# One layer of a chunk-causal encoder on one core: sums of a gathered tile move from the output phase to the gate phase, and the first loads and the last normalisation are placed anew

## The reference

```python
s = einsum('thpd,hpkd->thpk', q, sub_keys)          # 8 heads, 2 halves, 128 keys
sv, si = top_k(s, 16)                               # then the 16 best of 256 sums
idx = i1 * 128 + i2 ; g = softmax(best sums)        # 8 x 16 experts for each token
a = g * gelu(einsum('tkd,td->tk', expert_u[idx], x))
out = einsum('tk,tkd->td', a, expert_v[idx])
```

## Time and profile before

| | us |
|---|---|
| median of three runs (lowest, highest) | 3660.91 (3656.52, 3666.24) |
| the profiled execution's own time | 3626.26 |
| its span | 3624.5 |

### The profile page before, as it was taken

One profiled execution on the slowest core, in us unless ns is written; L12 is line 12 of the kernel. 1 busy time (PEld: TensorE's weight loads), 2 busy tenths in 40 slices (PEclk: granted clock), 3 DMA queues, 4 the chain that ended last, 5 costly groups with the idle time before them and its releaser, 6 DMA issues. The chain is left out here.

```text
span 3624.5 us, 42794 instructions
## 1 busy us (share of the span) xinstructions
PE 3096.4 (85%) x16184; PEld 2401.6 (66%) x16184; DVE 2127.5 (59%) x4487; ACT 1195.0 (33%) x1931; POOL 1474.7 (41%) x1116
## 2 busy tenths in 40 slices
PE   4995989798879999999999998666468988999994
PEld 3874777677768778888777766444246656677773
DVE  4143774215432169888867776767366666655555
ACT  3212452304221143444333332887422212222221
POOL 3100002410210007555867677776545545433332
PEclk9997699899989999999999999888779999999997
DMA  4333003321322249988999999899999999999993
GB/s 157 103 100 131 1 14 127 116 87 53 134 87 71 61 167 409 347 333 326 409 410 410 409 411 406 326 396 392 394 329 360 362 354 354 365 325 323 324 324 137
DMA packets 368045, 937.45 MB, mean 259 GB/s; under 512 B 31440, under 2 KB 130264, under 8 KB 366816
## 3 DMA queue, kind: packets, MB, share of 16 engines
q0 software_dynamic: 147456, 536.94, 38.6%
q1 hardware_dynamic: 220384, 397.77, 30.9%
HBM read 827.60 MB, written 106.98 MB: 258 GB/s over the span
## 5 line engine op out<-in xcount | busy, mean ns | idle before, releaser
L1406 POOL DMA_INDIRECT ex_ring<-in_expert_v,ex_idxT_sb x406 | 468.9, 1155 | 429.1 <-PE ex_ps_v L1431 300.0
L1406 POOL DMA_INDIRECT ex_ring<-in_expert_u,ex_idx_sb x322 | 428.0, 1329 | 386.9 <-DVE ex_hg L1415 205.1
L1415 DVE CUSTOM_DVE_ANT_0 ex_ring<-ex_ring,ex_xg 128x1024 f32<-128x1024 f32 x322 | 385.0, 1220 | 118.9 <-DMA ex_ring<-in_expert_u,ex_idx_sb 117.7
L106 PE MATMUL eo_ps<-eo_v_hi_sb,aT_late_hi 128*128 128x512 f32 x1024 | 410.7, 401 | 28.1 <-DVE aT_late_lo L1979 28.1
L106 PE MATMUL ex_ps_h<-aT_late_hi,ex_uT_hi_sb 128*128 128x512 f32 x1024 | 412.6, 403 | 1.9 <-ACT ex_uT_lo_sb L1547 1.1
L107 PE MATMUL eo_ps<-eo_v_lo_sb,aT_late_hi 128*128 128x512 f32 x1024 | 402.8, 393 | 0.0
L108 PE MATMUL ex_ps_h<-aT_late_hi,ex_uT_lo_sb 128*128 128x512 f32 x1024 | 402.1, 393 | 0.0
L107 PE MATMUL ex_ps_h<-aT_late_lo,ex_uT_hi_sb 128*128 128x512 f32 x1024 | 401.2, 392 | 0.0
L108 PE MATMUL eo_ps<-eo_v_hi_sb,aT_late_lo 128*128 128x512 f32 x1024 | 401.1, 392 | 0.0
L1431 PE MATMUL ex_ps_v<-ex_ring,ex_w_sb 128*32 128x512 f32 x1624 | 266.4, 697 | 147.4 <-DMA ex_ring<-in_expert_v,ex_idxT_sb 118.7
L1986 DVE TENSOR_TENSOR eo_acc<-eo_acc,eo_ps 128x1024 f32<-128x1024 f32 x124 | 151.5, 1221 | 356.9 <-PE eo_ps L108 356.9
(11 more groups left out here) (328 smaller groups left out, 6609.7 us busy)
## 6 DMA issues: line engine op xcount, KB each, us to landing
ex_u_raw<-in_expert_u SPq DMA_DIRECT2D x128, 512.0 KB, 8.3
eo_v_raw<-in_expert_v SPq DMA_DIRECT2D x128, 512.0 KB, 6.6
act_d<-ex_act SPq DMA_DIRECT2D x128, 256.0 KB, 6.1
gate_d<-ex_gate SPq DMA_DIRECT2D x8, 4096.0 KB, 14.9
eo_g_raw<-gate_d SPq DMA_DIRECT2D x64, 512.0 KB, 6.7
eo_a_raw<-act_d SPq DMA_DIRECT2D x128, 256.0 KB, 5.4
h_d<-n_row SPq DMA_DIRECT2D x24, 512.0 KB, 2.6
pin_raw<-in_w_in SPq DMA_DIRECT2D x20, 512.0 KB, 3.9
```

The source lines that it names most:

```text
L106: pe.matmul(ps, l_hi, r_hi, start=first, stop=False)
L1406: pool.indirect_dma_start(rows(n), None, table, bass.IndirectOffsetOnAxis(at, 0)).then_inc(ring_in[slot[n]], 16)
L1415: dve.tensor_tensor_reduce(out=u, in0=u, in1=xg[:, j, :], scale=1.0, scalar=0.0, op0=ALU.mult, op1=ALU.add, accum_out=hg[:, j, k:k + 1]).t ...
```

## The change

Counts and places are new, no arithmetic is. In words:

- Expert phase: the first tile's indices are computed in step 8 (`picked`, cut out of `route`), and dots begin at step 9, not 12. The weights of the softmax stay where they were.
- Gate phase: 96 steps instead of 72, still 64 of them with gate work. The 64 dots lie in steps 0 to 39, tile 1's 32 values in steps 0 to 45, the turn to tile 2 in steps 44 to 50 (`TURN_G` = 48), and tile 2's 32 values, formerly in the output phase, in steps 50 to 95.
- Output phase: 96 dots in e = 0 to 59; no values before e = 68, and tile 3's 32 values in e = 68 to 111. The first four experts' rows are loaded without a wait, the v rows into `acc`, the activations into the two `v_raw` buffers. The residual rows are loaded in e = 4 to 7 into `acc`, and added by the first group's `add`.
- The four gathered tiles are normalised within groups 30 and 31. Behind the last matmul only the late tiles are left, each after its own `add`. Gain and bias go into ring slots.

```diff
-            STEPS_G = HOT_GROUPS + 8
+            STEPS_G, TURN_G = HOT_GROUPS + 32, 48
-            FIRST_DOT = 12
+            FIRST_DOT = 9
             DOTS_A, DOTS_G, DOTS_B = 352, 64, 96
-            VALS_A, VALS_G, VALS_B = P, P, 2 * P
+            VALS_A, VALS_G, VALS_B = P, 2 * P, P
+            LAST_VALS, LN_TILES = 112, GROUPS - 2
+            def dots_g(n):
+                first = 2 * (DOTS_G // 2)
+                return share(first, TURN_G - 8, n) if n < TURN_G - 8 else 0
+            def vals_g(n):
+                if n < TURN_G - 2:
+                    return share(P // 4, TURN_G - 2, n)
+                if n >= TURN_G + 2:
+                    return share(P // 4, STEPS_G - TURN_G - 2, n - TURN_G - 2)
+                return 0
+            def dots_b(e):
+                return share(DOTS_B, ETILES // 2 - 4, e) if e < ETILES // 2 - 4 else 0
+            def vals_b(e):
+                half = ETILES // 2
+                if half + GE <= e < LAST_VALS:
+                    return share(P // 4, LAST_VALS - half - GE, e - half - GE)
+                return 0
...
     def a_raw(e):
-        return a_sb[:, e % 2, :]
+        return v_sb[:, e // 2, e % 2 * DN:(e % 2 + 1) * DN] if e < GE else a_sb[:, e % 2, :]
     def v_raw(e):
-        return v_sb[:, e % 2, :]
+        return acc[:, e, :] if e < GE else v_sb[:, e % 2, :]
...
+    for e in range(GE):
+        sp.dma_start(v_raw(e), v_rows[e, :, :]).then_inc(first_in[e], 16)
+        sp.dma_start(a_raw(e), act_d[e, :, :]).then_inc(first_in[e], 16)
+        if e % 2 == 0:
+            load_gates(e // 2)
...
+        if e < 2 * GE:
+            t = e - GE
+            sp.wait_ge(v_lo_done, t + 1)
+            sp.dma_start(acc[:, t, :], resid[(GT + t) * P:(GT + t + 1) * P, :]).then_inc(row_in[t], 16)
...
     if q == 0:
-        dve.tensor_copy(acc[:, t, :], ps[t % 2][:])
+        dve.wait_ge(row_in[t], 16)
+        dve.scalar_tensor_tensor(acc[:, t, :], acc[:, t, :], ALPHA, ps[t % 2][:], ALU.mult, ALU.add)
...
+    if LN_TILES <= q < LN_TILES + GT // 2:
+        j = 2 * (q - LN_TILES) + x // 2
+        if x % 2 == 0:
+            dve.wait_ge(sum_g, j + 1)
+            ln.statistics(dve, j, whole_row(j))
+        else:
+            ln.scale(dve, j)
+        if x % 2 == 0 and j >= 1:
+            ln.times_gain(dve, j - 1, whole_row(j - 1))
...
+    for t in range(DT):
+        add(GROUPS - 1, t)
+        dve.wait_ge(added[t % 2], 2 * (GROUPS - 1) + t // 2 + 1)
+        ln.statistics(dve, GT + t, whole_row(GT + t))
+        ln.times_gain(dve, GT + t - 1, whole_row(GT + t - 1))
+        ln.scale(dve, GT + t)
```

More of the change, by code:

```diff
@@ L1311, in expert_stages @@
             for n in range(STEPS_G):
-                for _ in range(share(DOTS_G, STEPS_G, n)):
+                for _ in range(dots_g(n)):
                     gathers.append(("u", nu))
                     nu += 1
-                for _ in range(4 * share(VALS_G // 4, STEPS_G, n)):
+                for _ in range(4 * vals_g(n)):
                     gathers.append(("v", nv))
@@ L1368, in expert_stages @@
             row_in = [sem(f"eo_row_in{i}") for i in range(DT)]
-            sum_done, stored = sem("eo_sum"), sem("eo_stored")
+            first_in = [sem(f"eo_first_in{i}") for i in range(GE)]
+            stored = sem("eo_stored")
             with ExitStack() as whole:
@@ L1855, in _ @@
                                         one_hot(n + 2)
-                                    for _ in range(share(DOTS_G, STEPS_G, n)):
+                                    for _ in range(dots_g(n)):
                                         dot(dve, done)
                                         done += 1
-                                weigh(dve, 2)
+                                    if n == TURN_G - 3:
+                                        weigh(dve, 2)
+                                    if n == TURN_G:
+                                        add_residual(dve, 1)
+                                        spread_weights(dve, 2)
                             @block.tensor
@@ L1878, in _ @@
                                         gates(n)
-                                    for _ in range(share(VALS_G // 4, STEPS_G, n)):
+                                    if n == TURN_G:
+                                        weight_transpose(pe, 2)
+                                    for _ in range(vals_g(n)):
                                         values(pe, done)
@@ L1884, in expert_stages @@
                     sb, pb = local(stage)
-                    ln = RowNorm("eo_ln", sb, gain, bias, rows=(spreads[:, 0, :], spreads[:, 1, :]))
+                    ln = RowNorm("eo_ln", sb, gain, bias, rows=(ring[:, 0, :], ring[:, 1, :]))
                     acc = sb("eo_acc", [P, DT, D])
@@ L1929, in _ @@
+                                if e == LN_TILES * GE:
                                     sp.wait_ge(val_done, GT * P // 4)
@@ L1994, in _ @@
                                 for x in range(GE):
[L1995 to L1997 removed]
+                                    multiply(q * GE + x)
+                                    low_parts(q * GE + x)
                                     if q >= 1:
                                         add(q - 1, x)
[L2000 to L2003 removed]
+                                    for _ in range(dots_b(q * GE + x)):
+                                        dot(dve, done)
+                                        done += 1
@@ L2043, in _ @@
                                     last.then_inc(out_mm[t % 2], 1)
-                                    for _ in range(share(VALS_B // 4, ETILES, q * GE + t)):
+                                    for _ in range(vals_b(q * GE + t)):
                                         values(pe, done)
```

109 lines of the change are left out of this document (50 added, 59 removed).

## The result

Timed side by side on the chip, 20 executions each, the changed kernel took 3667.07 us (median; 3654.97 to 3687.74) and the kernel before 3657.43 (3641.0 to 3670.12). The ratio over these executions is 1.0039, 95% interval 1.0022 to 1.0057, which is 14 us slower (8 to 21; the two medians alone lie 9.6 apart), where 9.5 us faster was forecast. A second comparison gave 1.0033 (1.0017 to 1.0049), 12 us.

The account below looks back on a forecast made before the run. DMA bytes bound the later expert phase and the gate phase, TensorE the output phase's second half. Expert -6, gate +164, output -132 and end -35.5 sum to -9.5: 3651 us against the median, range 3620 to 3690.

Parts of the forecast that it names:

- the price of the gate phase: Gate phase: 128 added gathers each cost their bytes, 1.28 us at 410 GB/s, +163.8 us, taken as +164.
- as at 391: Gate phase: bound of +172 us if every byte costs as at 391 GB/s.
- The third rival: Gate phase: tile 2's values wait for slots; at 6.4 us a set 28 more, +18, 3679 us; chance 0.13.
- The +14: Whole kernel, if the DMA limit were about 358 GB/s: 1.46 us a gather, gate phase +187; no chance of its own.
- The turn: Gate phase, steps 46 to 49 without values: ScalarE takes 16 to 18 us, the DMA has 22 us of work.
- The last two groups: End of the output phase: normalisation adds 3.4 us to VectorE in two steps, 10.5 of 11.15; 1 us added.
- The fourth rival: Groups 30 and 31: normalisation does not hide; at 2 us a tile lost, +8, so -1.5, 3659 us; chance 0.06.
- the output phase's first 15 groups: Groups 0 to 14: VectorE level with TensorE, 22.9 us a group, 343.5 us; bounds 22.3 and 25.7.
- the second rival: Output phase: the two raw buffers bind from a landing of 7.8; with 9.5, +42, so +32, 3693 us; chance 0.11.
- The end: Behind the last matmul: 13.3 us instead of 48.8, difference -35.5.
- The start: Output phase start: first matmul 26 us after the first issue, between 20 and 29, where it was 28.6.
- waits of values in triples: Output phase, groups 17 to 27: values wait for v gathers, 1.5 us short in each of 8 triples, +12; bounds 0 and 35.

Follow-up runs that it names:

- after2: The changed kernel, unchanged, run again for a second trace; ratio 1.0033 to the kernel before.

## Why the prediction was wrong, step by step

**The step that failed is the price of the gate phase:** "Since the DMA is saturated there, each costs its bytes: 1.28 us at 410 GB/s, +163.8". The growth was 179 us in the mean of all traces (183 by those of the first table, 168 to 194 by single pairs), 1.40 a gather, at the upper bound of 180.

The evidence for saturation was a DMA share of 1.00, but the rate beside it was 391 and not 410, and I priced the added bytes at the rate of another phase. The missing 5% was lost time, not other work's bytes. Over the whole phase, 2260.9 to 2620.7, the kernel before moved 377 GB/s; 67.1 MB at that rate are 178 us. The changed phase ran at about the same rate, 366 to 379 and some 375 in the mean, so its losses grew with its bytes.

That the stores' bursts and the slots are part of them is shown by the experiments; how, is my reading: behind a store the 13 slots land late and together, and the DMA has less to do until they are spread again. My bound "as at 391" (+172) took one window, without the phase's beginning and end, and the loss in it as constant; in that window the changed kernel ran at 370 to 383. By the timed ratios 14 slots give 14 us back, dots in the turn 7 (inside the intervals), both together 15, and pieces another 19; with all three the price is 164.

The third rival, slots, had the right kind of loss, at 28 us instead of some 14. (Its worse case, 7.7 us a set, is 57 us above the forecast, so +47 in all, and not the +57 that stands there.) The +14 that the prediction works out from a lower limit of the DMA is the measured figure by chance: the whole gate phase moved 366 GB/s or more in every trace with 13 slots, and 398 with pieces.

**The turn** was reckoned to have DMA work throughout, 22 us of it against 16 to 18 for four steps. I had miscounted the steps: `share(32, 46, 0)` is 0, so step 50 has no set of values either, and from the last set of tile 1, in step 45, to the first of tile 2, in step 51, TensorE's list has the gate work of six steps (46 to 51). ScalarE, which paces them at some 4.1 us each, was busy 20.0 of the 20 us from 2620 to 2640. The gap was 26 us (2606 to 2632), and 23 to 24 in the other four traces of the same phase; GpSimd was cut off for 19.3 us of it, and the DMA ran dry for 6 to 7 (share 0.28 from 2625 to 2635; 0.30 from 2608 to 2617 in after2). I had given such a gap 8 us in the bound only, which was its size.

**The last two groups:** "I add 1 for it". It was 11 to 14 (96 us by the adds, where 84.5 and 81.6 are had). The fourth rival had the place right, VectorE's list with waits on ScalarE, and the price at 8; that ScalarE's list holds back the high part, and that the bias addition on GpSimd stretches a low part by 2.15 us, I had not seen. The first could have been read from the order of ScalarE's list. The second stood in my rows, misread: the sum of 3.27 us at 3609.15 began 0.16 us after an addition of GpSimd that I had not put beside it,

```profile
3608.99 2.35 POOL L217 TENSOR_TENSOR eo_acc<-eo_acc,ex_w_sb 128x1024 f32<-128x1024 f32 x1 [4.18 <-DVE eo_acc L211]
```

and ended 1.08 us behind it, as the stretched low parts do. All four sums of 3.27 us lie so. I had put their length down to the product's place in SBUF instead of PSUM; an operation with both inputs in SBUF takes 1.22 as well where GpSimd makes no such addition (L1977 in the earlier trace rows).

**Right:** the output phase's first 15 groups were 347.8 us between the adds of group 0 and 15, first step at the low clock included (343.5 predicted; 344 to 353 in the other traces with the move), with VectorE level with TensorE as reckoned. The loads into two raw buffers did not bind; v rows landed in 7.0 us median in after2, below the 7.8 from which the second rival decides. The end was 13.3 to the tenth. The expert phase gave 8 for 6. The start won about 1 us, not 3: the first matmul came 27.3 us after the first issue in one trace and 28.4 in the other, for 28.6 before.

**Wrong, without effect:** waits of values in triples were put at 12 us; TensorE waited 0.9 us in all of groups 16 to 28. A group without values takes 21.8 and a set 2.1, not 22.3 and 1.85: the same 26.0 divided otherwise. The 12 us too many here hid part of the 11 to 14 too few in the last groups; the phase as a whole came to 833 for 822.8.

The range, 3620 to 3690, held the time. The error is one of sign: -9.5 for +14, of which the gate phase is 15 to 19 and the last groups some 10.

## What to carry to other kernels

A DMA share of 1.00 does not say that the phase runs at the chip's rate. In the changed kernel the share is 1.00 at 368 GB/s in one window (3260 to 3540), and in the kernel before it is 1.00 at 391. Compare GB/s with the best stretch of the same trace: what is missing there was paid again here by all that was moved in. Before moving work, price it at the rate of the whole receiving phase, its beginning and end included, and look first for what makes the losses; a large store beside a slotted ring is worth trying in pieces. Count the steps of a gap from what `share` returns and not from the bounds that it is given. Where an instruction is longer than its like, look at what the other engines do beside it. And where a list in order is given extra work, read what stands behind each new wait: here an activation that waited held the next tile's input.

## What the runs showed of the hardware that was not expected

- The 4 MB stores land in 15.6 us (median), and cutting them into 1 MB pieces raised a mixed phase from 385 to 409 GB/s in the same window, and shortened it from 529.1 to 512.0 us at the same bytes.
- A 128x1024 subtraction of two SBUF tiles on VectorE took 3.37 to 3.42 us instead of 1.22 while GpSimd added two SBUF tiles (2.65 to 2.78 instead of 2.40 us for GpSimd), and ended 1.08 us behind GpSimd's addition each time. An add of 128x1024 with one input in PSUM took 1.22 beside the same addition.
- Executions of one kernel in one comparison differ by up to 29 us (3641.0 to 3670.12), its median differs between comparisons (3657.43, and 3632 to 3637 in four others), and the same gate phase took 536.5 to 553.7 us in five traces. Differences of a few us between phases need more than one trace of each.
